# Output-bias products moved between experts, token count loaded ahead of the loop, last store in three parts, in a hybrid S5 / sparse-attention / mixture-of-experts block

## The reference

```python
def moe(h, w_router, b_router, w_moe_in, b_moe_in, w_moe_out, b_moe_out):
    logits = hf @ w_router + b_router
    vals, idx = lax.top_k(logits, 4)
    wts = jax.nn.softmax(vals, axis=-1)
    gates = jnp.sum(jax.nn.one_hot(idx, 32) * wts[..., None], axis=1)
    for e in range(32):
        z = hf @ w_moe_in[e] + b_moe_in[e]
        zg = jnp.minimum(z[:, ::2], 7.0)
        zl = jnp.clip(z[:, 1::2], -7.0, 7.0)
        act = zg * jax.nn.sigmoid(1.702 * zg) * (zl + 1.0)
        out = out + gates[:, e:e + 1] * (act @ w_moe_out[e] + b_moe_out[e])
x = x + moe(rms_norm(x, norm2_g), ...)
return rms_norm(x, norm_f_g)
```

## Time and profile before

| | us |
|---|---|
| median of 3 runs | 1242.6 (1241.57 to 1244.19) |
| the profiled execution's own time | 1242.14 |
| its span | 1240.3 |
| PE busy | 1141.2 |
| DVE, ACT, POOL busy | 358.9, 162.0, 93.1 |
| read from HBM | 433.52 MB |

### The profile page before, as it was taken

The page is one execution under the profiler, slowest core; times in us unless marked ns, Lnnn a source line. Parts: engine busy times, 40 slices in busy tenths (PEclk is TensorE's granted clock), DMA queues, the critical chain, the costliest instruction groups (busy, mean ns, idle before and its releaser), DMA issues.

```text
span 1240.3 us, 14037 instructions
## 1 busy us (share of the span) xinstructions
PE 1141.2 (92%) x5406; PEld 498.4 (40%) x5406; DVE 358.9 (29%) x718; ACT 162.0 (13%) x307; POOL 93.1 (8%) x69
## 2 busy tenths in 40 slices
PE   7786959998999999999999999999999999999996
PEld 6775727876333333333333333323232233222322
DVE  4989957222211122111112111111111111111112
ACT  5000134413100001000000010000000000000002
POOL 4745710000000000000000000000000000000000
PEclk9988989999999999999999999999999999999998
DMA  7522352378999998999999999999999999999994
GB/s 217 176 68 68 103 203 96 108 299 321 387 426 422 426 408 332 424 425 425 424 424 426 423 427 422 427 423 427 423 426 423 426 424 425 425 425 425 425 424 202
DMA packets 89084, 434.98 MB, mean 351 GB/s; under 512 B 13528, under 2 KB 36384, under 8 KB 39904
## 3 DMA queue, kind: packets, MB, share of 16 engines
q1 hardware_dynamic: 88480, 433.47, 85.6%
q10 hardware_dynamic: 576, 1.13, 0.3%
HBM read 433.52 MB, written 1.05 MB: 350 GB/s over the span
## 4 chain that ended last, share of the span: by engine, by line
PE 53%; DMA 19%; SPq 13%; DVE 7%; issue 3%; ACT 2%; POOL 1%; POOLq 0%; DVEq 0%
DMA ring<-in_w_moe_in 19%; PE ps L1444 18%; PE ps L1487 13%; SPq L440 11%; PE ps L1419 3%; PE ps L1169 3%; PE ps L1402 3%; DVE ring L753 3%; PE ps L1222 3%; PE ps L1353 2%; DVE ring L882 2%; PE ps L1454 1%; PE ps L1471 1%; PE ps L1343 1%; DVE late L915 1%
## 5 line engine op out<-in xcount | busy, mean ns | idle before, releaser
L1444 PE MATMUL ps<-ring,late 128*64 128x512 f32 x1024 | 234.0, 597 | 16.5 <-DMA ring<-in_w_moe_in 16.1
L1081 DVE TENSOR_SCALAR late<-ps 128x512 f32<-128x512 f32 x32 | 22.1, 691 | 708.0 <-PE ps L1444 708.0
L1487 PE MATMUL ps<-ring,late 128*64 128x512 f32 x896 | 198.5, 594 | 0.2
L1444 PEld LDWEIGHTS ps<-ring,late 128*64 128x64 f32 x1024 | 68.8, 136 | 177.2 <-issue 126.1
L1444 PE MATMUL ps<-wbuf,late 128*64 128x512 f32 x512 | 116.5, 596 | 0.0
L1487 PEld LDWEIGHTS ps<-ring,late 128*64 128x64 f32 x896 | 62.8, 137 | 122.8 <-issue 119.1
L716 ACT ACTIVATE late<-late 128x512 f32<-128x512 f32 x32 | 20.1, 630 | 531.0 <-DVE late L1081 531.0
L1169 PE MATMUL ps<-x_t,wbuf 128*128 128x256 f32 x320 | 70.7, 380 | 2.7 <-ACT ring L671 1.7
L1444 PEld LDWEIGHTS ps<-wbuf,late 128*64 128x64 f32 x512 | 35.1, 137 | 77.3 <-issue 75.0
L1169 PEld LDWEIGHTS ps<-x_t,wbuf 128*128 128x128 f32 x320 | 60.4, 190 | 11.8 <-issue 3.8
L1419 PE MATMUL ps<-late 64*128 64x512 f32 x256 | 63.6, 615 | 0.8 <-ACT late L723 0.8
(11 more groups left out here) (209 smaller groups left out, 954.2 us busy)
## 6 DMA issues: line engine op xcount, KB each, us to landing
ring<-in_w_moe_in SPq DMA_DIRECT2D x128, 1024.0 KB, 26.0
ring<-in_w_moe_out SPq DMA_DIRECT2D x112, 1024.0 KB, 23.8
wbuf<-in_w_moe_in SPq DMA_DIRECT2D x64, 1024.0 KB, 26.3
late<-in_w_moe_in SPq DMA_DIRECT2D x16, 1024.0 KB, 26.8
mixed<-in_w_moe_in SPq DMA_DIRECT2D x16, 1024.0 KB, 27.1
x_t<-in_w_moe_in SPq DMA_DIRECT2D x16, 1024.0 KB, 25.5
late<-in_w_moe_out SPq DMA_DIRECT2D x16, 1024.0 KB, 26.1
x<-in_w_moe_in SPq DMA_DIRECT2D x16, 1024.0 KB, 25.8
```

The source lines that it names most:

```text
L1081: ve.tensor_scalar(gate_z, z[:, 0], LIMIT, None, ALU.min).then_inc(z_gate, 1)
L1444: i = pe.matmul(ps[r, n // 2, :], h_sel[:, k % 4, k // 4, :], w[:, 512 * n:512 * n + 512], start=(k == 0), stop=(k == KD - 1))
L1487: i = pe.matmul(ps[64 * q:64 * q + SLOTS, 2, :], act_tile(k), w[:, 512 * q:512 * q + 512], start=(k == 0), stop=(k == KF - 1))
```

## The change

Three edits. The 4 output-bias products are issued in expert 1 and no more in expert 31 (`out_bias` in `body`). Every engine loads the token count into its register before its loop over the experts (SP: before its loop of loads; PE: between experts 1 and 2; ACT and DVE: between experts 0 and 1), and only the branch is left behind it. The last scaling of tokens 128 to 255 is split: ACT takes columns 0 to 511, and DVE columns 512 to 1023 ahead of its own tile; the output is stored in three parts in the order (tokens 128 to 255, columns 512 to 1023), (tokens 128 to 255, columns 0 to 511), (tokens 0 to 127).

```diff
         def passes(eng, one_pass):
-            one_pass(0, 0)
-            eng.wait_ge(flag_ok, 1)
-            most = eng.value_load(flag[0:1, 0:1], min_val=0, max_val=T)
+            held = []
+            def most_tokens():
+                eng.wait_ge(flag_ok, 1)
+                held.append(eng.value_load(flag[0:1, 0:1], min_val=0, max_val=T))
+            one_pass(0, 0, most_tokens)
+            most = held[0]
             with eng.If(most > SLOTS):
...
@@ sync
                     for n in range(NW):
                         load_chunk(LEAD + 1, n, 1)
+                if before_loop:
+                    before_loop()
                 with sp.Fori(LEAD // 2 + 1 if isinstance(c, int) else 0, NE // 2) as m:
...
-            for t in range(TT):
-                sp.wait_ge(out_ready[t], 1)
-                sp.dma_start(out[t * P:(t + 1) * P, :], final[:, t, :]).then_inc(stored, 16)
-            sp.wait_ge(stored, 16 * TT)
+            for n, (t, at, w) in ((2, (1, 512, 512)), (1, (1, 0, 512)), (0, (0, 0, D))):
+                sp.wait_ge(out_ready[n], 1)
+                sp.dma_start(out[t * P:(t + 1) * P, at:at + w], final[:, t, at:at + w]).then_inc(stored, 16)
+            sp.wait_ge(stored, 16 * 3)
@@ scalar
                 body(first)
+                if before_loop:
+                    before_loop()
                 with ac.Fori(1, NE - 1) as e:
...
-            ac.activation(final[:, 1, :], final[:, 1, :], ACT.Copy, scale=stat[:, 7:8]).then_inc(out_ready[1], 1)
+            ac.activation(final[:, 1, 0:512], final[:, 1, 0:512], ACT.Copy, scale=stat[:, 7:8]).then_inc(out_ready[1], 1)
@@ vector
                 body(first, 0)
+                if before_loop:
+                    before_loop()
                 with ve.Fori(1, NE - 1) as e:
...
             ve.wait_ge(under_gains, 4)
+            ve.tensor_scalar(final[:, 1, 512:D], final[:, 1, 512:D], stat[:, 7:8], None, ALU.mult).then_inc(out_ready[2], 1)
             ve.tensor_scalar(final[:, 0, :], final[:, 0, :], stat[:, 6:7], None, ALU.mult).then_inc(out_ready[0], 1)
@@ tensor
-                        if tail and isinstance(c, int) and k < 2 * TT:
+                        if out_bias and isinstance(c, int) and k < 2 * TT:
...
                 body(first, pairs, 0, head=True)
-                body(first + 1, pairs, 1)
+                body(first + 1, pairs, 1, out_bias=True)
+                if before_loop:
+                    before_loop()
                 with pe.Fori(1, NE // 2 - 1) as m:
```

More of the change, by code:

```diff
@@ L287, in build @@
         sum_open, squared, tile_ok, first_sum_ok, under_gains = sem("sum_open"), sem("squared"), sem("tile_ok"), sem("first_sum_ok"), sem("under_gains")
-        out_ready, stored = [sem(f"out_ready{t}") for t in range(TT)], sem("stored")
+        out_ready, stored = [sem(f"out_ready{n}") for n in range(3)], sem("stored")
         v_chain, a_chain, g_chain = sem("v_chain"), sem("a_chain"), sem("g_chain")
@@ L433, in _, with one_pass @@
                 sp.dma_start(extra_place(n), expert_chunk(1, n)).then_inc(extra_in[n], 16)
-            def one_pass(c, first):
+            def one_pass(c, first, before_loop=None):
                 def load_chunk(e, n, odd):
@@ L1422, in scatter, with body @@
                             i.then_inc(done, 1)
-                def body(j, pair, odd, head=False, tail=False):
+                def body(j, pair, odd, head=False, tail=False, out_bias=False):
                     def weights(k):
```

## The result

| | before | after |
|---|---|---|
| median of 15 runs, us | 1242.85 (1241.29 to 1245.21) | 1246.1 (1243.65 to 1248.15) |
| ratio | | 1.0023, 95% interval 1.0014 to 1.0031 |
| profiled execution's span, us | 1240.3 | 1244.5 |

The changed kernel is slower by 0.23%, or 2.8 us (the difference of the means; the medians lie 3.25 us apart), with an interval of 1.7 to 3.9 us. The forecast was +1.8 us and 1244.4. The time of 1246.1 lies in the stated range, 0.1 us under its upper end, and 0.5 us above the narrower range (1243.2 to 1245.6) that the prediction gave its forecast.

The account below looks back on a forecast made before the run. PE was taken to bound the early experts and the stream of weights the late ones. Terms of +4.68 - 1.76 - 0.8 - 0.3 = +1.8 us on 1242.6 gave 1244.4 us, range 1242.0 to 1246.2.

Parts of the forecast that it names:

- The last weights land at a fixed distance from PE's use of chunk 9 of expert 5: After the gap at 470 us the weight stream never stops; its last chunk lands 752 us after SP's issue at 470.28.
- The first rival: Expert 1's 4.68 us go into PE's lead and don't reach the end: -2.9 us, 1239.7 us; chance 0.09.
- +4.68 us in expert 1: The four added bias products delay PE's use of chunk 9 of expert 5, and the whole stream, by 4.68 us.
- -1.76 us in expert 31: Without the products PE saves 4.68 us, but chunk 7's landing lets it keep only 1.76 us.
- The two halves: The bias products' move into expert 1 (+4.68) and out of expert 31 (-1.76), together +2.92 us.
- Two signs: In expert 31, waits of about half a microsecond on chunks 4 to 7, and a `w_moe_in` part 17.8 us long.
- -0.8 us for the token count: In the tail, PE's far branch starts about 0.8 us earlier with the load gone; its 3.62 us run from its start.
- The second and third rivals: Second (0.12): branch's end tied to PE's last product, 1245.2 us; third (0.07): load ahead of expert 2 delays PE, 1245.4 us.
- -0.3 us for the last scaling and the stores: At the end, splitting the scaling lets stores begin 0.33 us earlier and end about 0.3 us earlier.
- The sum: All terms over the whole kernel: +4.68 - 1.76 - 0.8 - 0.3 = +1.8 us, giving 1244.4 us.

Follow-up runs that it names:

- 1: Against the kernel before, only the four output-bias products moved from expert 31 to expert 1: 1246.77 against 1244.03 us, ratio 1.0024.
- 2: Against the kernel before, the bias products done in expert 1 and again in expert 31: 1247.94 against 1244.03 us, ratio 1.0032.
- 5: Against the kernel before, only the bias products moved, from expert 31 to expert 30: 1241.76 against 1244.01 us, ratio 0.9982.
- 3: Against the kernel before, only the token count loaded ahead of the loops, as in the change: 1243.06 against 1244.03 us, ratio 0.9993.
- 4: Against the kernel before, only the last scaling and the stores split, as in the change: 1243.38 against 1244.03 us, ratio 0.9998.
- 8: The changed kernel with SP's written-out order kept up to expert 12, against the kernel before: 1236.64 against 1244.01 us, ratio 0.9938.
- 11: The changed kernel with SP's written-out order kept up to expert 16, against the kernel before: 1235.77 against 1243.82 us, ratio 0.9932.
- LEAD 6: The kernel before as it stands, with SP's written-out load order up to expert 6: 1244.01 us in the rounds of the LEAD 12 run.
- LEAD 12: SP's written-out load order kept up to expert 12 instead of 6; in the kernel before, 1237.51 against 1244.01 us, ratio 0.9942.

## Why the prediction was right, step by step

- *The last weights land at a fixed distance from PE's use of chunk 9 of expert 5.* Shown by 1 and 2: 4.6 us in expert 1 appear whole at SP's issue in both, and whole at the end in 2. The first rival would have let the times of 1 and 2 fall or stay. The stretch in which nothing is moved grew from 7 to some 10 us and not to the 11 foreseen, because 1.5 us of the delay were already lost near 366 us. Chunk 11 of expert 31 lands at 1203.49 + 25.8 = 1229.3 us, 889.2 us behind the start of expert 1; before it was 1222.3, 884.3 behind it. That is +4.9, 0.2 more than foreseen.
- *+4.68 us in expert 1.* Measured 19.56 instead of 14.90 us: +4.66, and +4.64 at SP's issue.
- *-1.76 us in expert 31.* Chunk 7 landed at 1192.25 + 27.1 = 1219.35 in the changed kernel, 7.03 us later than before, and was started 5.32 us later: 1.7 us kept. The tail's gain again in 5, 1.7 us by the trace. The two halves together came to +3.16 us at chunk 7, 0.24 more than foreseen; the landings scatter by that much, as the text allowed (in 1 the same distance grew by 2.8). Two signs were off in size: the waits began at chunk 3 and not 4, and expert 31's `w_moe_in` part took 18.6 us instead of the 17.8 named (17.9 in 1).
- *-0.8 us for the token count.* -1.0 in the profiled pair, -0.8 as the mean of the executions in 3. The branch's end goes with its start: 3.62 us before, 3.55 us after, with a start 0.9 us earlier against the scatter. The Trainium skill, Runtime: NRT & Kernel Launch, section Instruction fetch mechanics, says that a taken branch to a target outside the window already held must wait for a fetch. That the time runs from the branch's start agrees with it; that the 3.6 us are such a fetch is not shown by any run here. The second and third rivals fall by experiment 3.
- *-0.3 us for the last scaling and the stores.* A term that was slightly too large: -0.17 in the profiled pair and in 4, -0.2 over the fourteen executions. ACT's half took 0.72 us and not 0.6, and DVE's half 0.49 and not 0.42, so the first issue came 0.5 us behind the start of the scaling instead of 0.45, and the third 1.4 us instead of 1.25. It landed 3.0 us later, 4.4 us behind the start of the scaling, as foreseen; the span's end follows 0.1 us later than worked out, which is about the rounding of these rows.
- *The sum.* +1.8 foreseen, +2.04 from expert 1's start on in the profiled pair. The means say +2.8 (1.7 to 3.9), the medians +3.25. The first quarter of the span, which no edit touches, moves by more than this sum from one execution to the next, so the times alone can't tell +1.8 from +2.8. The mechanism and its terms are borne out; that the time itself still fell inside the stated range, by 0.1 us, is owed in part to that scatter and to the width of the range.
- *Missing in the prediction:* the second place at which the stream runs low, near 366 us. It cost nothing here, because what is lost there is time that the gap at 470 us takes up (the loss at the gap grew by only 2.9 us, that near 366 by 1.5); it showed only when the gap was removed, in 8 and 11.

## What to carry to other kernels

Where a stream of weights bounds the end, ask when it last stood still and for whom: when it was PE that the stream waited for, work added on PE ahead of that moment costs its full time, however idle the memory looks, and work removed behind it is worth only PE's distance from the landings. Work that can stand anywhere belongs where its engine waits for data. And a pause in the stream that comes from the order of the issues is worth more than all of the tail's trimming: here one constant gave 6.5 us, and the three edits of the tail in their best places 2.5.

## What the runs showed that I had not expected

- The pause at the change of SP's order doesn't vanish with a later change: 8.0 us lost at LEAD 6, 3.4 at 8, 1.0 to 1.9 at 12, 0.9 to 1.3 at 16. From LEAD 12 on PE is itself waiting for chunks there (18.0 us busy in the 20 us from 640). Why some 1 to 2 us stay is not settled.
- The first 340 us scatter by some 4 us between executions, with PE's mean granted clock there at 0.95 and 0.93 in the two kernels compared; a change of 2 us can be read from one pair of traces only by distances from a point behind that stretch.
